# The order of the query tiles in forgetting attention of a two-layer hybrid encoder on one Trainium2 core

## The reference, cut to what matters

```python
def block(args):
    q_blk, c_blk, i = args
    s = jnp.einsum('bqhd,bkhd->bhqk', q_blk, k).astype(jnp.float32) * scale
    s = s + c_blk[..., None] - cum_k[:, :, None, :]
    q_pos = i * FOX_BLOCK + jnp.arange(FOX_BLOCK)
    s = jnp.where(key_pos[None, :] <= q_pos[:, None], s, NEG)
    p = jax.nn.softmax(s, axis=-1).astype(v.dtype)
    return jnp.einsum('bhqk,bkhd->bqhd', p, v)
out = lax.map(block, (qb, cb, jnp.arange(nb)))
```

## Time and profile before

| | |
|---|---|
| median of three executions | 1901.37 us (1900.83 to 1903.24) |
| the profiled execution, its own time | 1902.85 us |
| its span, first to last instruction | 1901.0 us |
| mean granted TensorE clock | 0.996 of full speed |
| TensorE busy | 98% of the span |
| forgetting stretch of layer 0, `scores(8)` to the end of the last `attend` | 486.27 to 548.85 us |
| the same stretch of layer 1 | from 1420.97 us |

### The profile page before, as it was taken

One profiled execution on the slowest core, in us unless ns is written; L12 is line 12 of the kernel. 1 busy time (PEld: TensorE's weight loads), 2 busy tenths in 40 slices (PEclk: granted clock), 3 DMA queues, 4 the chain that ended last, 5 costly groups with the idle time before them and its releaser, 6 DMA issues.

```text
span 1901.0 us, 25245 instructions
## 1 busy us (share of the span) xinstructions
PE 1869.0 (98%) x9472; PEld 1544.2 (81%) x9472; DVE 986.6 (52%) x1350; ACT 710.7 (37%) x1112; POOL 204.5 (11%) x420
## 2 busy tenths in 40 slices
PE   8999999999999999999999999999999999999998
PEld 7888888887668888888888888889876788888887
DVE  5664442387667544442376544325876574444323
ACT  5332332254654333332253323223656453333321
POOL 2741000013100000000047110000130000000000
PEclk9999999999999999999999999999999999999999
DMA  6334333243213333333333443333511323333331
GB/s 181 103 115 129 95 113 105 75 139 112 57 56 89 92 97 99 99 111 102 92 103 94 139 101 100 109 102 103 158 52 50 90 67 100 99 94 106 107 92 44
DMA packets 330957, 188.61 MB, mean 99 GB/s; under 512 B 6996, under 2 KB 325432, under 8 KB 329848
## 3 DMA queue, kind: packets, MB, share of 16 engines
q1 hardware_dynamic: 324008, 168.13, 30.7%
q0 software_dynamic: 5824, 18.79, 3.4%
q10 hardware_dynamic: 1040, 0.52, 0.1%
HBM read 175.72 MB, written 11.67 MB: 99 GB/s over the span
## 4 chain that ended last, share of the span: by engine, by line
PE 91%; DVE 6%; ACT 2%; issue 1%; DMA 0%; DVEq 0%; ACTq 0%
PE ps L590 18%; PE ps L592 18%; PE ps L591 18%; PE ps L792 8%; PE ps L790 8%; PE ps L791 8%; PE ps L646 1%; PE ps L648 1%; PE ps L653 1%; PE ps L750 1%; PE ps L749 1%; PE ps L751 1%; PE ps L620 1%; PE ps L631 1%; PE ps L622 1%
## 5 line engine op out<-in xcount | busy, mean ns | idle before, releaser
L1643 DVE TENSOR_TENSOR wl<-raw,wh 128x1024 fp32r<-128x1024 f32 (+1 forms) x260 | 344.5, 1326 | 738.3 <-ACT wh L1152 737.4
L590 PE MATMUL ps<-xh,wh 128*128 128x512 f32 x1536 | 606.7, 395 | 7.5 <-DVEq L1881 6.3
L592 PE MATMUL ps<-xh,wl 128*128 128x512 f32 x1536 | 599.0, 390 | 0.0
L591 PE MATMUL ps<-xl,wh 128*128 128x512 f32 x1536 | 598.5, 390 | 0.0
L1152 ACT ACTIVATE wh<-raw 128x1024 fp32r<-128x1024 f32 (+1 forms) x260 | 295.8, 1139 | 637.7 <-PE ps L792 324.6
L590 PEld LDWEIGHTS ps<-xh,wh 128*128 128x128 f32 x1536 | 289.2, 188 | 72.8 <-DVEq L1881 7.9
L592 PEld LDWEIGHTS ps<-xh,wl 128*128 128x128 f32 x1536 | 288.7, 188 | 61.0
L591 PEld LDWEIGHTS ps<-xl,wh 128*128 128x128 f32 x1536 | 289.1, 188 | 60.1 <-issue 1.7
L790 PE MATMUL ps<-Hh,wh 128*128 128x512 f32 x638 | 248.4, 389 | 0.0
L792 PE MATMUL ps<-Hh,wl 128*128 128x512 f32 x638 | 248.2, 389 | 0.0
L791 PE MATMUL ps<-Hl,wh 128*128 128x512 f32 x638 | 248.2, 389 | 0.0
(11 more groups left out here) (382 smaller groups left out, 2038.9 us busy)
## 6 DMA issues: line engine op xcount, KB each, us to landing
raw<-in_ffn_up SPq DMA_DIRECT2D x88, 512.0 KB, 3.8
raw<-in_ffn_down SPq DMA_DIRECT2D x64, 704.0 KB, 4.5
raw<-in_ffn_gate SPq DMA_DIRECT2D x87, 512.0 KB, 3.9
raw<-in_w_in SPq DMA_DIRECT2D x28, 512.0 KB, 4.0
raw<-in_w_out SPq DMA_DIRECT2D x16, 512.0 KB, 3.7
xrow<-in_x SPq DMA_DIRECT2D x2, 1024.0 KB, 8.6
ssm_t<-evict POOLq DMA_DIRECT2D x8, 256.0 KB, 3.2
ssm_v<-evict POOLq DMA_DIRECT2D x8, 256.0 KB, 2.7
```

The lines of the kernel that those rows point to most:

```text
L590: pe.matmul(bank, w_tile(True, slot, kw), xh[:, kx, :], start=first, stop=False)
L591: pe.matmul(bank, w_tile(True, slot, kw), xl[:, kx, :], start=False, stop=False)
L592: return pe.matmul(bank, w_tile(False, slot, kw), xh[:, kx, :], start=False, stop=last)
L1643: V.tensor_tensor(w_low(slot, k0, nk), raw[:, slot4, 0:nk - k0, :], w_high(slot, k0, nk).bitcast(F32), ALU.subtract).then_inc(w_split, 1)
```

## The change

The list of forgetting items runs through the query tiles in falling order, so that the lengths are 512, 512, 384, 384, 256, 256, 128, 128 keys for each head pair. The waits that belong to the first tile in the list move from i == 0 to i == TOK - 1, which is 3. No instruction is added or removed.

```diff
-ITEMS += [("fox", j, 2 * j + a, i, list(range(i + 1))) for j in range(FOX_HEADS // 2) for i in range(TOK) for a in range(2)]
+ITEMS += [("fox", j, 2 * j + a, i, list(range(i + 1))) for j in range(FOX_HEADS // 2) for i in reversed(range(TOK)) for a in range(2)]
...
-                        if i == 0 and h % 2 == 0:
+                        if i == TOK - 1 and h % 2 == 0:
                             pe.wait_ge(fox_rdy, l * 4 + 2 * (j + 1))
                             pe.wait_ge(aug_ld, (l + 1) * (2 * FOX_HEADS * 16))
...
-                    if i == 0 and kind == "fox":
+                    opens = i == (TOK - 1 if kind == "fox" else 0)
+                    if opens and kind == "fox":
                         pe.wait_ge(v_rdy, l * 3 + j + 2)
-                    if i == 0 and pr == 1:
+                    if opens and pr == 1:
                         pe.wait_ge(y0_rdy, l * 2 + 2)
-                    if i == 0 and pr >= 2:
+                    if opens and pr >= 2:
```

## The result

The changed kernel took 1905.34 us (median of 20 executions, 1902.66 to 1908.06), the kernel before 1901.41 (20 executions). The ratio is 1.0018, with a 95% interval of 1.0012 to 1.0024: slower by 3.9 us. Timed again later, the ratio was 1.0020 (1.0011 to 1.0029). The forecast was 1902.1, with a range of 1899.0 to 1905.6; the time is in the range, near its upper end and close to the 1905.2 of the slower rival.

What follows compares the result with a forecast made beforehand. TensorE, busy for 98% of the span, was taken to bound the kernel. Waits of -0.8 us and clock of +1.55 gave +0.75, added to the median 1901.37 for 1902.1 us, with a range of 1899.0 to 1905.6.

Steps and rivals of the forecast that it cites:

- slower rival: Behind steps 18 to 20 the lower clock lasts twice as long, 3.1 us per layer: 1905.2 us, chance 0.15.
- piece of step 10: Projection piece waiting for VectorE behind item 9's maximum: starts 4.24 us after scores(9), not 3.21; net +0.2 us per layer.
- gate product: Step 12, waiting on a ScalarE chain from item 8's copy: starts 0.77 us later, net +0.35 us per layer.
- branch sum's wait: Step 13, 0.96 us for VectorE's addition: nearly all of it goes, net -0.85 us per layer.
- the attend: Step 19, items 14 and 15: starts 12.28 us after item 11's transposes, not 11.92; wait grows from 1.54 to about 2.4.
- the output piece: First one, step 19: starts at 13.94 us, not 13.03, with a new 0.8 us wait; steps 15 to 19 net +0.9.
- attend of step 25: Starts 4.45 us after scores(23), not 5.64, as item 23 shortens; steps 24 and 25 net -0.7 us per layer.
- wait of step 27: TensorE waits for item 23's copy, which shrinks from 0.60 to about 0.28 us: net -0.3 us per layer.
- steps 20 to 23: Each edge keeps at least 0.5 us of slack, so 0 change; waits there would show the forecast wrong.
- Their sum: Net of the changed waits in the forgetting stretch: -0.4 us per layer, -0.8 us for two layers.
- The clock: TensorE's granted clock falls behind step 19 in both layers, not one: +1.55 us, from -1.6 to +4.7.
- heavy items 16 and 17: With 512 keys each, they delay step 19's attend and first output piece; steps 15 to 19 net +0.9 us per layer.

Runs made afterwards that it cites:

- filled kernels: Unused bf16 matmuls on constants ahead of step 19's attend: kernel before 0.9995, first pair falling 1.0008, second pair falling 0.9979, the change 0.9992.
- filling runs: Unused bf16 matmuls ahead of step 19's attend: 12 in the changed kernel, 1900.57 us (0.9992); 8 in the kernel before, 1901.38 us (0.9995).
- second-pair kernel: Only the second head pair in falling order, the first rising as in the kernel before: 1898.21 us, ratio 0.9981.
- first-pair kernel: Only the first head pair in falling order, the second rising as in the kernel before: 1909.69 us, ratio 1.0038.
- earlier split: Weight split of output unit 1 moved from step 17 to 16: on the changed kernel 1902.95 us (1.0006), with only the second pair falling 1896.63 us (0.9975).
- second look: Both kernels timed and profiled again without filling, nothing else changed: changed kernel 1905.62 us, kernel before 1901.65 us.

## Why the prediction was right, and the size of one term wrong

**Waits, step by step.** The ends of the chains held to a few hundredths. The piece of step 10 was put 4.24 us behind the scores of item 9: it is 496.61 - 492.37 = 4.24. The gate product was put 0.77 later than 1.73 us behind the transposes of item 8; it is 2.49 (504.92 to 507.41). The branch sum's wait, expected nearly gone, is gone. From the transposes of item 11, at 517.35, the attend was put at 12.28 and the output piece at 13.94: they are at 12.25 and 13.93, with waits of 2.22 and 0.66 (about 2.4 and 0.8 were forecast). The attend of step 25 was put 4.45 behind scores(23) and is at 4.43. The wait of step 27 fell from 0.69 to 0.37. No wait appeared at keys, values or decay rows, and none in steps 20 to 23.

**Their sum** was -0.8 us. The filled kernels, whose stretches are all at clock 1.00, give 2 x (62.34 - 62.54) = -0.4 us, right in sign and half in size. The times give -0.03% (-0.6 us), which is within their intervals. The listed waits of layer 0 fell by 0.9 us (7.2 to 6.3) where the stretch fell by 0.2, so the sum of waits is not the measure of the gain.

**The clock** is the term that was mis-sized. It stood as +1.55, from one fall more, as long as the one of layer 1. The filling runs put it at about 4: filling gives 4.9 us in the changed kernel and 1.0 in the kernel before. The place was right (behind step 19, in both layers), but the profiled stretches hold only 2.1 to 2.5 us of these 3.9, and where the rest lies is open. The wrong step was to take "the value nearest to the longest wait measured": one fall of known length per layer. The clock stays low longer there, at 0.95 over the stretch in three of the four layers seen. Why is not shown. In those three it is low already at the attend, within the 2.2 us wait; in the fourth, at 0.97, it fell only behind the second wait. Behind the wait come four short matmuls and four transposes. The second-pair kernel waited 2.0 us, has sixteen matmuls in that attend, and stands at 0.97 in both layers.

A second slip made the forecast low. The term counts one fall in the kernel before, which its profiled execution has (1902.85 us), but the sum was added to the median of three, 1.48 lower. On 1902.85 the same sum gives 1903.6.

So the forecast moved by +0.75 and the kernel by +3.9; the time is in the range because the range took in the slower rival. That rival described what happened, a lower clock held twice as long, with its place and 1905.2 us, and it was given 0.15. That 1905.2 is so near the median is partly luck: it counted 3.1 us of clock per layer, and the profiled stretches hold 1.6 to 2.2. With 4.9 - 1.0 = 3.9 for the clock, the sum would have been -0.8 + 3.9 = +3.1, or +3.5 with the measured -0.4, against the +3.9 of the medians.

The Trainium skill, "TensorE: Matmul & The Clock Gate", section "HAM oscillation — how this bites in real kernels", says that a kernel whose matmul bursts are parted by waits can be brought back to the half clock at each of them, and that the work should be arranged so that the array stays warm. The rows agree for step 19: 0.97 and 0.95 in the stretches of the change, 1.00 with the wait filled. The waits of the page's example are longer than any here; that waits of 1.5 to 2.2 us are enough is shown by these rows alone. The fall around 1090 us doesn't fit, since it comes with no wait in the trace.

**What the walk could not see** is which half of the change did what. I ascribed the cost to the heavy items 16 and 17 and the gain to step 13. The runs show the reverse for the pairs: falling order in the first pair loses 0.95 us per layer, in the second it gains 1.15. The branch sum's wait of step 13 is no gain: it goes in the first-pair kernel, and the waits at step 19 grow from 1.5 to 2.3 and 0.5.

## What to carry to other kernels

When a stretch has one late chain, ask what starts it. Here long items ahead of the gate product cost 2.68 us there and gave back only 1.75 behind it. Long items between it and the output piece cost 1.75 and saved 2.91 behind. The middle was not free, only the cheapest place. So long items belong between and short ones ahead and behind, which may mean a different order for each half of a list. When TensorE's waits are moved together, count the granted clock as a cost of its own, from more than one execution, and test it by filling the wait with idle matmuls.

## What was not expected of the hardware

- Adding 12 unused matmuls per layer made the changed kernel 4.9 us faster (1.0018 to 0.9992), with the attend as far behind the gate product as before.
- The longest wait doesn't tell whether the clock falls: after one wait of 1.5 us (kernel before) it fell in one layer of two, after two waits of 0.9 with short transposes between (changed kernel, earlier split) in both, and after a wait of 0.8 (second pair falling, earlier split) in neither.
- The clock also fell with no wait in the trace. In the profiled execution of the kernel before this was around 1090 us, behind 32 matmuls of 32 columns that took 3.8 us from the first start to the next matmul's, with TensorE shown busy throughout. In its second look the same row of matmuls brought no fall (1.00 from 1085 to 1100 us).

```profile
1088.00:1089.00 1.00, 1.00 (x11) 1.00 (x10) 1.00 (x2) 0.00 (x0) 0.00 (x0) 1.00 0.00 0
1089.00:1090.00 1.00, 1.00 (x7) 1.00 (x7) 0.16 (x1) 0.63 (x1) 0.00 (x0) 0.57 0.14 40
1090.00:1091.00 1.00, 1.00 (x3) 0.81 (x4) 0.00 (x0) 0.38 (x1) 0.43 (x1) 0.50 0.82 240
```
